# The prologue by feature chunk: wide row sums, the first layer's scale and shift chunk by chunk, and the first two up steps taken jointly along the contraction

## The reference, cut to what matters

```python
def rms_norm(x, w=None):
    y = x * lax.rsqrt(jnp.mean(x * x, axis=-1, keepdims=True) + EPS)
    return y * w if w is not None else y

def ada_in(x, g, m, s):
    return rms_norm(x, g) * (1 + m[:, 3 * s + 1][:, None, :]) + m[:, 3 * s][:, None, :]

def swiglu(h, w_in, w_out):
    g, u = jnp.split(h @ w_in, 2, axis=-1)
    return (jax.nn.silu(g) * u) @ w_out

m_lat = (silu(c) @ ada_w[l] + ada_b[l]).reshape(-1, 9, D_MODEL)       # shift, scale, gate, three times
m_ctx = (silu(c_ctx)[None] @ ada_w[l] + ada_b[l]).reshape(1, 9, D_MODEL)
x  = x  + 0.5 * gate(m_lat, 0) * swiglu(ada_in(x,  norm_w[l, 0], m_lat, 0), ffn_w_in[l, 0], ffn_w_out[l, 0])
xc = xc + 0.5 * gate(m_ctx, 0) * swiglu(ada_in(xc, norm_w[l, 0], m_ctx, 0), ffn_w_in[l, 0], ffn_w_out[l, 0])
# ... then the mixers and the other FFNs, twice; the result is rms_norm(x, final_norm_w)
```

## Time and profile before

| | before |
|---|---|
| median of 3 runs | 2191.33 us |
| lowest and highest | 2187.29 and 2192.61 us |
| the profiled execution | 2188.84 us, its span 2187.2 us |
| TensorE matmul busy | 2058.6 us, 94% of the span |
| VectorE / ScalarE / GpSimd busy | 60% / 35% / 5% |
| mean DMA rate | 126 GB/s |

### The profile page before, as it was taken

The page is one execution under the profiler, slowest core; times in us unless marked ns, Lnnn a source line. Parts: engine busy times, 40 slices in busy tenths (PEclk is TensorE's granted clock), DMA queues, the critical chain, the costliest instruction groups (busy, mean ns, idle before and its releaser), DMA issues.

```text
span 2187.2 us, 28339 instructions
## 1 busy us (share of the span) xinstructions
PE 2058.6 (94%) x10430; PEld 1748.2 (80%) x10430; DVE 1319.4 (60%) x1865; ACT 761.3 (35%) x972; POOL 112.9 (5%) x173
## 2 busy tenths in 40 slices
PE   6999999997898978999999999999998999898998
PEld 6788888885687877988888888888887788677887
DVE  4677677756544675687667863363346524766666
ACT  2432122323444232432122243212233225845444
POOL 1010001000000230010000000000000000100000
PEclk9999999998898998999999999999999999999999
DMA  8355555531020000265555532243233223123554
GB/s 311 111 193 178 182 179 172 174 107 58 3 93 30 1 1 29 95 214 186 179 179 179 191 114 96 100 157 123 81 106 116 79 95 135 58 94 138 177 192 131
DMA packets 53994, 275.45 MB, mean 126 GB/s; under 512 B 6928, under 2 KB 8208, under 8 KB 36496
## 3 DMA queue, kind: packets, MB, share of 16 engines
q1 hardware_dynamic: 34032, 200.86, 26.6%
q0 software_dynamic: 19728, 72.88, 10.1%
q10 hardware_dynamic: 144, 0.46, 0.1%
HBM read 273.13 MB, written 1.05 MB: 125 GB/s over the span
## 4 chain that ended last, share of the span: by engine, by line
PE 85%; DVE 7%; ACT 4%; issue 2%; DMA 1%; POOL 0%; SPq 0%; ACTq 0%; DVEq 0%
PE ps L947 15%; PE ps L948 15%; PE ps L949 15%; PE ps L959 8%; PE ps L1100 5%; PE ps L1101 5%; PE ps L1102 5%; PE ps L960 4%; PE ps L1138 1%; DVE w_lo L654 1%; ACT w_hi L456 1%; PE ps L1724 1%; PE ps L1720 1%; DMA const<-in_const 1%; PE ps L1060 1%
## 5 line engine op out<-in xcount | busy, mean ns | idle before, releaser
L947 PE MATMUL ps<-h_parts,w_lo 128*128 128x512 f32 (+1 forms) x1576 | 601.2, 381 | 8.4 <-DVE h_parts L776 4.4
L948 PE MATMUL ps<-h_parts,w_hi 128*128 128x512 f32 (+1 forms) x1576 | 596.7, 379 | 0.0
L949 PE MATMUL ps<-h_parts,w_hi 128*128 128x512 f32 (+1 forms) x1576 | 596.3, 378 | 0.0
L456 ACT ACTIVATE w_hi<-w_raw 128x2048 fp32r<-128x2048 f32 (+3 forms) x207 | 353.9, 1710 | 508.6 <-PE ps L1102 261.7
L654 DVE TENSOR_TENSOR w_lo<-w_raw,w_hi 128x2048 fp32r<-128x2048 f32 (+3 forms) x207 | 421.9, 2038 | 136.8 <-ACT w_hi L456 136.4
L663 DVE SCALAR_TENSOR_TENSOR ada_product<-ada_w,silu_c 128x1024 bf16<-128x1024 f32 x272 | 332.7, 1223 | 45.2 <-DMA ada_w<-in_ada 14.7
L947 PEld LDWEIGHTS ps<-h_parts,w_lo 128*128 128x128 f32 x1576 | 299.8, 190 | 65.1 <-issue 5.3
L948 PEld LDWEIGHTS ps<-h_parts,w_hi 128*128 128x128 f32 x1576 | 299.6, 190 | 55.4 <-issue 1.4
L949 PEld LDWEIGHTS ps<-h_parts,w_hi 128*128 128x128 f32 x1576 | 299.5, 190 | 54.5
L468 ACT ACTIVATE sil<-ps 128x512 f32<-128x512 f32 x66 | 39.5, 598 | 488.3 <-PE ps L949 488.3
L959 PE MATMUL ps<-h_parts,w_hi 128*128 128x512 f32 x544 | 198.1, 407 | 6.3 <-DVE h_parts L860 2.5
(11 more groups left out here) (304 smaller groups left out, 2308.7 us busy)
## 6 DMA issues: line engine op xcount, KB each, us to landing
w_raw<-in_w_up SPq DMA_DIRECT2D x88, 1024.0 KB, 4.8
ada_w<-in_ada POOLq DMA_DIRECT2D x136, 512.0 KB, 3.9
w_raw<-in_w_down SPq DMA_DIRECT2D x32, 768.0 KB, 4.1
w_raw<-in_w_ret SPq DMA_DIRECT2D x24, 1024.0 KB, 4.8
w_raw<-in_w_down SPq DMA_DIRECT2D x32, 640.0 KB, 3.9
w_raw<-in_w_ab SPq DMA_DIRECT2D x14, 1024.0 KB, 4.8
w_raw<-in_w_ret_out SPq DMA_DIRECT2D x8, 1024.0 KB, 4.8
ada<-in_ada SPq DMA_DIRECT2D x8, 512.0 KB, 19.9
```

The costliest lines, as they stand in the source:

```text
L456: act.activation(w_hi[slot][:, 0:elems], w_raw[slot][:, 0:elems], ACT.Copy).then_inc(hi_ready, 1)
L947: pe.matmul(out, lo, rhs_hi(k), start=first and k == 0, stop=False)
L948: pe.matmul(out, hi, rhs_lo(k), start=False, stop=False)
L949: mm = pe.matmul(out, hi, rhs_hi(k), start=False, stop=last and k == nk - 1)
```

## The change

Data and order:

- `ada00` takes the place of `ada0` and of the eight shift tiles: eight transfers of 1 MB on SyncE's queue, one for each feature chunk n, each with the scale columns and the transposed shift columns of that chunk. `x` comes in four transfers, `const`'s first two blocks (identity and ones) in a small one of their own, and the first two weight steps stand before `ada00[0]` and `ada00[1]`. Small tables move to the GpSimd and ScalarE queues.
- TensorE first runs 16 matmuls of a zeroed bf16 tile. The row sums are eight fp32 products of the full 128x128 block of ones with 512 columns of squares, so that every partition holds the sums; ScalarE squares the even chunks, VectorE the odd ones; root and reciprocal are taken over 128x512 elements.
- GpSimd multiplies each chunk of `x` by the inverse.
- Scale and shift of chunk c are made by TensorE (`scale(c)`, eight calls of a two-column fp32 product) and VectorE (two multiplies with row sum, then two small operations), chunk by chunk, and each chunk's modulation follows at once.
- The first two up steps are taken together: for each contraction chunk k, the products of steps 0 and 1 (12 matmuls), then `scale(k + 2)`.

The diff, cut to its core:

```diff
     def sp_program(sp):
...
-        sp.dma_start(x[:], a["xT"]).then_inc(x_loaded, 16)
-        sp.dma_start(const[:], a["const"]).then_inc(x_loaded, 16)
+        for i in range(KD // 2):
+            sp.dma_start(x[:, 2 * i:2 * i + 2], a["xT"][:, 2 * i:2 * i + 2]).then_inc(x_loaded[i], 16)
+        sp.dma_start(const[:, 0:2 * P], a["const"][:, 0:2 * P]).then_inc(const_loaded, 16)
         for k in range(KD):
-            sp.dma_start(ada0[:, k, :], a["ada0"][k]).then_inc(ada0_ready[k], 16)
...
+            if k < 2:
+                sp.dma_start(w_raw[k][:, 0:ELEMS[k]], runs[0][4](k)).then_inc(raw_ready[k], 16)
+            sp.dma_start(ada00[:, k], a["ada00"][k]).then_inc(ada00_ready[k], 16)
...
     def pool_program(pool):
...
-        for t in range(ADA_SHIFT):
-            tile(t, t % 2, wait=t >= 2)
...
+        pool.dma_start(const[:, 2 * P:], a["const"][:, 2 * P:]).then_inc(loaded, 16)
...
+        pool.wait_ge(inverse_done, 1)
+        for c in range(KD):
+            if c >= 2:
+                pool.wait_ge(shifted, c - 1)
+            pool.tensor_tensor(prod[:, c % 2], x[:, c], rstd_wide[:], ALU.mult).then_inc(normed, 1)
+            if c >= KD - 2:
+                pool.wait_ge(ada00_ready[KD - 1], 16)
+                tile(ADA_START + c - KD + 2, c % 2, wait=False)
...
     def act_modulate(act, norm):
...
         def one(c, b):
+            if norm == "n00" and c == 1:
+                split_hi(act, 1, 1, ELEMS[1])
             act.wait_ge(normed, base_c + c + 1)
+            if norm == "n00":
+                act.wait_ge(first_mod, c + 1)
...
     def scalar_program(act):
...
-        for r in range(KD):
-            act_square(act, "n00", r, r % 2, ALL)
-        act_root(act, "n00", 0, 1.0 / D)
+        act.activation(warm_root[:], vecs[:, 2:3], ACT.Sqrt).then_inc(warmed, 1)
+        for r in range(0, KD, 2):
+            act.wait_ge(x_loaded[r // 2], 16)
+            if r >= 4:
+                act.wait_ge(ssq_done, r - 3)
+            act.activation(first_squares(r), x[:, r], ACT.Square).then_inc(even_squared, 1)
+        act.wait_ge(ssq_done, KD)
+        act.activation(root_wide[:], ps[:, NRM, :], ACT.Sqrt, bias=vecs[:, 2:3], scale=1.0 / D).then_inc(root_done, 1)
+        split_hi(act, 0, 0, ELEMS[0])
+        act_modulate(act, "n00")
         act.wait_ge(loaded, 16 * RESIDENT)
-        split_hi(act, 0, 0, ELEMS[0])
-        split_hi(act, 1, 1, ELEMS[1])
-        act_modulate(act, "n00")
...
     def vector_program(dve):
...
-        for t in range(ADA_SHIFT):
-            ada_tile(dve, t, t % 2)
...
+        dve.wait_ge(root_done, 1)
+        dve.reciprocal(rstd_wide[:], root_wide[:]).then_inc(inverse_done, 1)
...
+        def low(c):
+            dve.wait_ge(h_hi_done, c + 1)
+            dve.tensor_tensor(h_lo[:, c], sil[:, c % 2], h_hi[:, c].bitcast(F32), ALU.subtract).then_inc(h_lo_done, 1)
+
+        for c in range(KD):
+            dve.wait_ge(ada00_ready[c], 16)
+            for st in range(2):
+                if c or st:
+                    dve.wait_ge(first_dot, 2 * c + st)
+                dve.scalar_tensor_tensor(out=ada_product[:], in0=ada00[:, c, 1], scalar=1.0, in1=silu_c[:, st, :],
+                                         op0=ALU.mult, op1=ALU.mult, accum_out=mcol[:, st, c:c + 1]).then_inc(first_dot, 1)
+            dve.wait_ge(scale_made, c + 1)
+            dve.tensor_scalar(mod[:, 0, 0, :, c], ps[:, 5 + c % 2, 0:2], mod_tmp[:, 0, c:c + 1], norm_g[:, 0, c:c + 1],
+                              ALU.add, ALU.mult)
+            dve.wait_ge(first_dot, 2 * c + 2)
+            dve.tensor_scalar(mod[:, 0, 1, :, c], mcol[:, :, c], mbias[:, c:c + 1], None, ALU.add).then_inc(first_mod, 1)
+            if c < 2:
+                split_lo(dve, c, c, ELEMS[c])
+            if c:
+                low(c - 1)
+        low(KD - 1)
...
+    def pe_first_pairs(pe):
+        def scale(n):
+            pe.wait_ge(ada00_ready[n], 16)
+            if n >= 2:
+                pe.wait_ge(first_mod, n - 1)
+            for k in range(KD):
+                mm = pe.matmul(ps[:, 5 + n % 2, 0:2], ada00[:, n, 0, k * P:(k + 1) * P], c_cols[:, 2 * k:2 * k + 2],
+                               start=k == 0, stop=k == KD - 1)
+            mm.then_inc(scale_made, 1)
+
+        pe.wait_ge(c_silu, 2)
+        scale(0)
+        scale(1)
+        for k in range(KD):
+            for s in range(2):
+                if k == 0:
+                    pe_ready(pe, s)
+                pe.wait_ge(h_lo_done, k + 1)
+                for u in range(2):
+                    mm = products(pe, ps[:, 2 * s + u, :], s, u * D + k * P, 1, lambda _: h_hi[:, k, :],
+                                  lambda _: h_lo[:, k, :], k == 0, k == KD - 1)
+                if k == KD - 1:
+                    mm.then_inc(step_done, 1)
+            if k + 2 < KD:
+                scale(k + 2)
+        pe.wait_ge(loaded, 16 * RESIDENT)
...
     def tensor_program(pe):
-        pe.wait_ge(x_loaded, 32)
+
+        pe.wait_ge(idle_set, 1)
+        for _ in range(16):
+            pe.matmul(ps[:, 7, :], idle_tile[:, 0:P], idle_tile[:], start=True, stop=True)
+        pe.wait_ge(const_loaded, 16)
         for r in range(KD):
-            pe.wait_ge(sq_ready, r + 1)
-            pe_ssq(pe, "n00", r, prod[:, r % 2], 0).then_inc(ssq_done, 1)
...
+            pe.wait_ge((even_squared, odd_squared)[r % 2], r // 2 + 1)
+            pe.matmul(ps[:, NRM, :], ones, first_squares(r), start=r == 0, stop=r == KD - 1).then_inc(ssq_done, 1)
```

More of the change, by code:

```diff
@@ L175, in build @@
     hid_lo, hid_hi = hid_parts[:, 0], hid_parts[:, 1]
-    ada0, _ = put("ada0", [P, KD, D], at=at_r)
+    ada00, _ = put("ada00", [P, KD, 2, D], at=at_r)
+    root_wide, _ = put("root_wide", [P, T], at=at_r + 64 * 1024)
+    rstd_wide, _ = put("rstd_wide", [P, T], at=at_r + 66 * 1024)
+    idle_tile, _ = put("idle_tile", [P, T], BF16, at=at_r + 68 * 1024)
     c_cols = small[:, 440:440 + 2 * KD]
@@ L348, in build @@
     seam_before = {n: i for i, n in enumerate(SEAMS)}
-    squares_before, count = {}, 0
-    for n in norms:
+    squares_before, count = {"n00": 0}, 0
+    for n in norms[1:]:
         squares_before[n] = count
@@ L430, in tile @@
                 pool.wait_ge(ada_dot, 2 * t - 2)
-            index = t if isinstance(t, int) and t < ADA_SHIFT else t - ADA_START + ADA_SHIFT
+            index = t - ADA_START
             pool.dma_start(ada_w[:, slot, :], a["ada"][bass.ds(index, 1)].rearrange("a p n -> (a p) n")) \
                 .then_inc(ada_ready[slot], 16)
-        for t in range(ADA_SHIFT):
-            tile(t, t % 2, wait=t >= 2)
-        for t in range(2):
-            pool.wait_ge(ada_dot, 2 * (ADA_SHIFT - 1 + t))
-            tile(ADA_START + t, t, wait=False)
+        for dst, key in ((conv_w[:], "conv_w"), (vecs[:, 0:1], "dn_norm"), (vecs[:, 1:2], "subln")):
+            pool.dma_start(dst, a[key]).then_inc(loaded, 16)
+        pool.dma_start(const[:, 2 * P:], a["const"][:, 2 * P:]).then_inc(loaded, 16)
+        pool.dma_start(gate_in[:, 0, :], a["a_log"][0, :].partition_broadcast(P)).then_inc(loaded, 16)
+        pool.dma_start(gate_in[:, 1, :], a["dt_bias"][0, :].partition_broadcast(P)).then_inc(loaded, 16)
+        pool.dma_start(small[:, 0:16], a["ret_decay"][0, :].partition_broadcast(P)).then_inc(loaded, 16)
+        pool.dma_start(small[:, 64:320], a["lam"][0, :].partition_broadcast(P)).then_inc(loaded, 16)
+        pool.wait_ge(inverse_done, 1)
[6 more added lines that the diff above has]
+                tile(ADA_START + c - KD + 2, c % 2, wait=False)
         with pool.Fori(0, (ADA_BEFORE_DN - ADA_START - 2) // 2) as i:
@@ L496, in act_square @@
         n = cols.stop - cols.start
[L497 to L500, removed]
+        if not (isinstance(r, int) and r < 2):
             act.wait_ge(sq_added, adds_before(norm) + r - 2)
-        out = sil[:, 0, 0:n] if norm != "n00" and isinstance(r, int) and r == 0 else prod[:, slot, 0:n]
+        out = sil[:, 0, 0:n] if isinstance(r, int) and r == 0 else prod[:, slot, 0:n]
         act.activation(out, x[:, bass.ds(r, 1), cols].rearrange("p a n -> p (a n)"),
@@ L595, in one @@
                            ACT.Copy).then_inc(h_hi_done, 1)
+        if norm == "n00":
+            for c in range(KD):
+                one(c, c % 2)
+            return
         one(0, 0)
@@ L879, in vector_program @@
         for slot in range(2):
-            dve.memset(sil[:, slot], 0.0).then_inc(acc_free, 1)
-        dve.wait_ge(c_silu, 2)
-        for t in range(ADA_SHIFT):
-            ada_tile(dve, t, t % 2)
[L884 to L887, removed]
+            dve.memset(vecs[:, 4 + slot:5 + slot], 0.0).then_inc(acc_free, 1)
+        dve.memset(idle_tile[:], 0.0).then_inc(idle_set, 1)
+        for r in range(1, KD, 2):
+            dve.wait_ge(x_loaded[r // 2], 16)
+            if r >= 4:
+                dve.wait_ge(ssq_done, r - 3)
+            dve.tensor_tensor(first_squares(r), x[:, r], x[:, r], ALU.mult).then_inc(odd_squared, 1)
```

(6 more changed lines are left out.)

76 lines of the change are left out of this document (30 added, 46 removed).

## The result

| | before | after |
|---|---|---|
| median | 2191.97 us (6 runs) | 2206.53 us (6 runs) |
| lowest, highest | 2185.73, 2194.10 | 2205.41, 2209.57 |
| ratio | | 1.0077, 95% interval 1.0065 to 1.0089 |
| the profiled execution | 2188.84, span 2187.2 | 2206.85, span 2205.1 |

The change makes the kernel 0.8% slower: the two medians lie 14.6 us apart, and the ratio makes it 16.9 us (14.2 to 19.5 by its interval). The forecast was 2207. The page after: TensorE's busy time is what it was, and the clock (second line, in tenths, 40 slices) is low in the first two slices. That second line can't be held against the page before: there it prints 9 in these slices, though the weight loads up to 58.9 us took the 333 ns of the low level.

The account below looks back on a forecast made before the run. TensorE, busy 94%, bounds the kernel; step 2's start decides. Chunk 0 at 41.1, plus 51 and 7.7, gives 99.9; seam 3.8 and low clock 1.8 give 105.5 against 89.5: 16 us later, 2207 us, range 2189 to 2219.

Parts of the forecast that it names:

- The loop is serial: Prologue loop: products, scale, small operations, `low`, products never overlap; six rounds of 8.5 us make 51 us.
- The clock starts each burst low and rises within it: TensorE in the loop: each 12-matmul burst starts low, mostly rises late, falls again before the next; round 8.5 us.
- The round: One pass of the prologue loop per chunk: 8.5 us forecast, 9.9 with the clock all low, 5.9 all high.
- S: Eight two-column scale calls on TensorE per round: 3.4 us low, 1.8 high, 2.4 as a mean.
- P: The 12 matmuls of one chunk's products per round: 5.1 us low, 2.7 high, 4.7 forecast.
- the rest: Per round, last record's end, handovers, VectorE's small operations and `low`: 1.4 us.
- The dates in front: Prologue before the loop: constants land at about 15.4, inverse at 29.1, `h_lo` of chunk 0 done at 41.1 us.
- R: Date in the prologue when the reciprocal is done and the inverse is there: 29.1 us.
- the last two bursts: Products 6 and 7 at the loop's end, following without a wait: 7.7 us, both steps done at 99.9.
- The seam: Behind the joint steps TensorE idles 3.8 us while step 2's weights are split; a low start loses 1.8 more.
- The first: Rival: clock stays high through the loop, round 5.9 us, step 2 2 to 4 us earlier, 2188 to 2189; chance 0.14.
- The transfers: Rival: chunk transfers pace the loop at 0.12 MB/us against 0.41, time some 2212 us; chance 0.03.

Follow-up runs that it names:

- the runs with scales ahead: The changed kernel with three or four scales made ahead of the first products instead of two: 2185.50 us (ratio 0.9984) and 2182.70 us (0.9968).
- four scales ahead: The changed kernel with scale(0) to scale(3) made ahead of the first products, using a fourth PSUM bank: 2182.70 us, ratio 0.9968 to the kernel before.
- the zeros: The changed kernel with five matmuls of a zeroed bf16 tile behind each scale(k+2) of the loop: 2200.37 us, ratio 1.0052 to the kernel before.
- the joint form alone: The kernel before with only its first two up steps taken jointly chunk by chunk, prologue untouched: 2196.30 us, ratio 1.0025.
- steps apart: The changed kernel with only step 0 taken chunk by chunk and step 1 whole behind it: 2200.70 us, ratio 1.0055 to the kernel before.

## Why the prediction was right, step by step

- *The loop is serial.* Right, and shown by the runs with scales ahead: the same work in another order is 22 us sooner. From the first product to the end of both steps it took 53.8 us, and 31.1 with four scales ahead.
- *The clock starts each burst low and rises within it.* Right in the main, and priced by the zeros: 10 us. Four bursts of six start low, and the other two fall within 0.9 us; it rises within five of six, and behind the third only in its narrow calls. The round was 7.55 us, not 8.5. The term that was mis-sized is S: I took a mean of 2.4 us for the eight narrow calls, with the clock low in part of them; they took 1.69 in five rounds and 2.02 in one, since the clock rises before the burst's end and falls only behind the narrow calls. P was 4.55 against 4.7, the rest 1.25 against 1.4. Six rounds: 45.3, not 51.
- *The dates in front.* 4.6 us too early: 41.1 against 45.7. The constants landed at 17.9, not 15.4. I had scaled the landing by bytes. The DMA rates of the kernel after make it 4.1 MB moved by 15.2 us, about as I had reckoned, and 5.2 MB by 17.9: some of what was issued behind the constants had moved before they were all there. What held them up is not settled, and the run that issues them first shows only what it costs. Behind the reciprocal, GpSimd's multiplications cost VectorE 2.4 us more than the 0.7 I charged: from R it took 14.4, not 12.0, and 12.0 with the multiplications on VectorE, their own 0.7 each included. The sums took 9.2 us (9.3), the reciprocal 3.35 (3.2 to 3.4).
- These two errors, +4.6 and -5.7, and +0.7 in the last two bursts cancel, and both steps ended at 99.5 (forecast 99.9). That part of the hit is luck. The sign doesn't hang on it, but the size does: the first alone would have made the loss 21 us, the second alone 10.
- *The seam*: 3.6 us (forecast 3.8), step 2 at 103.1 (103.7), and 1.8 us lost at the low level (1.8), which comes 1 us into step 2 and not at its start. Right; the joint form alone cost the kernel before 5.0 us of date.
- *The rivals.* The first (clock high throughout) was made nearly true by the zeros: from the second burst on its round is 5.8 us, and even so the down date is 5.3 us later than before. Against the 3.7 us earlier that I had put for it, with no low start, the first product came 4.9 later, the six rounds took 1.3 more since the first burst was low, and the low level in step 2 cost 3.0 where I had 0 to 1.8. With the front alone put right, this rival would not have been on the other side. The transfers never set the pace.

By dates, the change's 15.3 us are these. The first product comes 19.1 us earlier. From there to the end of both steps it takes 53.8 us instead of 24.8, 29.0 more: 11.5 of them go with the zeros, so they are the clock, and 17.5 remain, which are the narrow calls (six times 1.7) and the waits between the bursts (six times 1.2). The seam adds 3.6 us and the low level behind it 1.8. The late constants and the contention with GpSimd are in the date of the first product: it could have come earlier still.

## What to carry to other kernels

Where two engines pass a chunk to and fro, write down for each wait which earlier instruction of the same in-order queue stands ahead of its releaser: a distance of two was serial here; a distance of three had no waits, and cost one PSUM bank. An early first product is worth nothing by itself; the date to compare is when the common work behind starts. And a stretch of narrow matmuls joined to a wait is worse than either: the 1.7 us of narrow calls alone did not bring the clock down, nor did 1.0 us of waiting alone; 1.7 us of narrow calls with 1.1 us of waiting behind them did.

## What the runs showed of the hardware

- Between bursts of twelve wide fp32r matmuls, 1.7 us of two-column calls left the clock at its high level in every round (four ahead: 4.55 us a round). With 1.1 us of waiting behind the calls it fell in every round, in the wait or up to 0.9 us behind it; matmuls of zeros in that gap held it at 1.00.
- The same narrow product has two speeds: 16 records in 1.84 us at the high level, 3.41 at the low one (kernel after, steps apart).
- A GpSimd multiplication of two SBUF tensors beside VectorE's two-input operation slowed both: VectorE's 1.23 us became 2.15, and 0.69 became 1.75; GpSimd's took 1.6 to 2.2, against 1.27 for its like in the earlier trace rows.
- VectorE's reciprocal over 512 fp32 columns took 3.35 us, 6.5 ns a column, against 0.69 for a subtraction.
- The same code of the mixer took 996 or 999 us, with the clock at 0.85 or 0.64 in one 8 us window. These 3 us are as large as many effects one would like to measure in the whole time.
